# Reordering the first stage of a two-block transformer kernel: x in two loads, the memory row one unit earlier

## The reference, cut to what matters

```python
h = rmsnorm(x, norm_mix[i])
proj = h @ a_w_in[i]
u, b_gate, c_gate, q_mem = split(proj, [CONV_WIDTH, 2 * CONV_WIDTH, 3 * CONV_WIDTH])
v = c_gate * u
conv = w[0] * vp[:, 0:s] + w[1] * vp[:, 1:s + 1] + w[2] * vp[:, 2:s + 2]
y_tok = b_gate * conv
mem_kv = rmsnorm(mem, mem_norm) @ w_mem_kv[i]
```

## Time and profile of the kernel before

| | |
|---|---|
| median of 3 runs | 934.93 us (933.76 to 939.04) |
| the profiled execution | 932.69 us, of which the span is 931.0 us |
| TensorE busy | 919.3 us, 99% |
| VectorE busy | 704.0 us, 76% |
| ScalarE busy | 549.9 us, 59% |
| granted TensorE clock | 0.999 of full speed |

### The profile page before, as it was taken

How to read it: one execution, slowest core, us unless ns; L and a number is a source line. 1 busy time by engine, 2 the same in 40 slices (tenths; PEclk the granted TensorE clock), 3 DMA queues, 4 the chain that set the end, 5 groups by cost and what they waited for, 6 DMA issues and landing times.

```text
span 931.0 us, 16864 instructions
## 1 busy us (share of the span) xinstructions
PE 919.3 (99%) x6163; PEld 813.4 (87%) x6163; DVE 704.0 (76%) x1284; ACT 549.9 (59%) x969; POOL 81.9 (9%) x105
## 2 busy tenths in 40 slices
PE   8999999999999999999999999999999999999997
PEld 8999888888888987888888888999889789999985
DVE  4978777767666777687766677998687887688975
ACT  5654465545455677665555546775654745477883
POOL 0000011111110000100000000000011005622200
PEclk9999999999999999999999999999999999999999
DMA  8665557766666332667655663544231685423312
GB/s 322 210 204 178 191 172 238 224 215 200 207 204 190 112 113 92 234 224 229 206 191 183 189 187 118 174 146 134 83 102 50 202 286 189 142 87 102 119 46 91
DMA packets 43726, 157.94 MB, mean 170 GB/s; under 512 B 5464, under 2 KB 6248, under 8 KB 42896
## 3 DMA queue, kind: packets, MB, share of 16 engines
q1 hardware_dynamic: 41520, 147.79, 48.6%
q0 software_dynamic: 1856, 8.58, 2.5%
q10 hardware_dynamic: 288, 0.72, 0.3%
HBM read 155.63 MB, written 1.05 MB: 168 GB/s over the span
## 4 chain that ended last, share of the span: by engine, by line
PE 89%; DVE 5%; ACT 3%; DMA 2%; issue 1%; SPq 0%; DVEq 0%; ACTq 0%
PE ps L758 15%; PE ps L543 9%; PE ps L544 8%; PE ps L545 8%; PE ps L756 8%; PE ps L598 7%; PE ps L602 7%; PE ps L600 7%; PE ps L753 2%; DMA raw<-stream_dram 2%; PE ps L1145 1%; DVE wl L1772 1%; PE ps L754 1%; PE ps L1099 1%; ACT wh L1231 1%
## 5 line engine op out<-in xcount | busy, mean ns | idle before, releaser
L1772 DVE TENSOR_TENSOR wl<-raw,wh 128x1024 fp32r<-128x1024 f32 x270 | 331.8, 1234 | 100.0 <-ACT wh L1399 50.5
L1231 ACT ACTIVATE wh<-raw 128x1024 fp32r<-128x1024 f32 x174 | 182.0, 1056 | 91.6 <-DMA raw<-stream_dram 83.3
L758 PE MATMUL ps<-hxa,wh 128*128 128x512 f32 x616 | 219.6, 396 | 0.0
L543 PE MATMUL ps<-hxa,wh 128*128 128x256 f32 x672 | 196.6, 293 | 1.8 <-DVE hxa L1783 0.9
L544 PE MATMUL ps<-hxa,wh 128*128 128x256 f32 x672 | 189.9, 283 | 0.0
L545 PE MATMUL ps<-hxa,wl 128*128 128x256 f32 x672 | 189.8, 282 | 0.0
L756 PE MATMUL ps<-hxa,wl 128*128 128x256 f32 x616 | 171.9, 279 | 0.0
L543 PEld LDWEIGHTS ps<-hxa,wh 128*128 128x128 f32 x672 | 128.3, 191 | 11.3 <-issue 7.0
L1399 ACT ACTIVATE wh<-raw 128x1024 fp32r<-128x1024 f32 x96 | 101.6, 1058 | 59.9 <-PE ps L758 21.7
L758 PEld LDWEIGHTS ps<-hxa,wh 128*128 128x128 f32 x616 | 115.6, 188 | 24.0
L544 PEld LDWEIGHTS ps<-hxa,wh 128*128 128x128 f32 x672 | 128.6, 191 | 0.1
(11 more groups left out here) (370 smaller groups left out, 1354.2 us busy)
## 6 DMA issues: line engine op xcount, KB each, us to landing
raw<-stream_dram SPq DMA_DIRECT2D x271, 512.0 KB, 4.1
biasm<-bias_dram POOLq DMA_DIRECT2D x12, 192.0 KB, 4.2
w<-w_dram POOLq DMA_DIRECT2D x1, 2048.0 KB, 10.8
mlw<-mlw_dram POOLq DMA_DIRECT2D x1, 1056.0 KB, 6.9
x<-x_dram SPq DMA_DIRECT2D x1, 1024.0 KB, 7.2
mem<-memT_dram SPq DMA_DIRECT2D x1, 1024.0 KB, 8.3
memx<-mem_dram SPq DMA_DIRECT2D x1, 1024.0 KB, 5.8
grow<-rows_dram POOLq DMA_DIRECT2D x2, 512.0 KB, 4.5
```

The costliest lines, as they stand in the source:

```text
L543: pe.matmul(o, wh[:, w_s, w_cols], act[hi], start=start, stop=False, skip_group_check=True)
L758: return pe.matmul(o, wh[:, s % RING, wc], hx[:, k, :, :], start=False, stop=(k == KC - 1), skip_group_check=True)
L1231: act.activation(wh[:, v % RING, :], raw[:, v % RAW, :], ACT.Copy).then_inc(wh_ready, 1)
L1772: dve.tensor_tensor(wl[:, s % RING, :], raw[:, s % RAW, :], wh[:, s % RING, :].bitcast(F32), ALU.subtract).then_inc(wl_ready, 1)
```

## The change

- **SP:** x is loaded in two transfers of 512 KB, tokens 0 to 127 and 128 to 255, with unit 4 between them; each has its own semaphore.
- **ACT:** the first square stands ahead of the split of unit 4, the second behind it. The two squares and the root of `memx` move from step 6 to step 5 of the loop and stand ahead of the high part of convolution 0; the high part of a convolution stands behind them in its step.
- **DVE:** the token row and the two queries are taken in step 1, ahead of the first low parts of the memory (before: step 2). Each of the first two convolutions is computed behind the low part of the weight unit of the next step (before: ahead of it) and directly followed by its own low part. The memory's reciprocal and diagonal stand in step 6 behind the low part of unit 10 (before: step 7, ahead of unit 11, behind the take of b of convolution 1).
- **PE:** the memory's row is made behind unit 8 (before: behind unit 9).

```diff
             load(RAW, RAW)
             sp.dma_start(ident[:], ident_d).then_inc(ident_landed, 16)
-            sp.dma_start(x[:], x_d).then_inc(x_landed, 16)
+            sp.dma_start(x[:, 0, :], x_d[:, 0, :]).then_inc(x_landed[0], 16)
             load(RAW + 1, RAW + 1)
+            sp.dma_start(x[:, 1, :], x_d[:, 1, :]).then_inc(x_landed[1], 16)
             load(RAW + 2, RAW + 2)
...
-                if e == ("K", 0, 1):
+                if e == ("K", 0, 0):
                     rrow(ROW_MEM, 2)
...
-            for u in range(2, 5):
+            for u in range(2, 4):
                 split(u)
-            act.wait_ge(x_landed, 16)
-            for t in range(2):
-                square(Q_A, t, ajunk)
+            act.wait_ge(x_landed[0], 16)
+            square(Q_A, 0, ajunk)
+            split(4)
+            act.wait_ge(x_landed[1], 16)
+            square(Q_A, 1, ajunk)
             root2(Q_A, 0)
...
-                if j and A_PRE[j - 1][0] == "c":
-                    high(t_y[:], A_PRE[j - 1][1], A_PRE[j - 1][1])
-                if j == 6:
+                if j == 5:
                     act.wait_ge(memx_landed, 16)
...
+                if j and A_PRE[j - 1][0] == "c":
+                    high(t_y[:], A_PRE[j - 1][1], A_PRE[j - 1][1])
...
-                if j == 7:
-                    dve.wait_ge(mstd_ready, 1)
-                    dve.reciprocal(mrt, mstd).then_inc(mrt_ready, 1)
-                    dve.wait_ge(mrt_ready, 1)
-                    diagonal(mrt)
...
                 if j:
                     ahead_of(PA[e], e)
+                if j == 6:
+                    dve.wait_ge(mstd_ready, 1)
+                    dve.reciprocal(mrt, mstd).then_inc(mrt_ready, 1)
+                    dve.wait_ge(mrt_ready, 1)
+                    diagonal(mrt)
                 if e in (("u", 1), ("K", 0, 0)):
                     done = 0 if e[0] == "u" else 1
+                    convolve(done)
                     low_part(t_y[:], done, Y_A_SLOTS.index(done))
-                if j == 2:
+                if j == 1:
                     rows(ROW_A, 0, R)
```

More of the change, by code:

```diff
@@ L374, in build @@
         xT_landed = [sem(f"xT_landed{i}") for i in range(2)]
-        x_landed, grow1_landed, grow2_landed = sem("x_landed"), sem("grow1_landed"), sem("grow2_landed")
+        x_landed = [sem("x_landed%d" % t) for t in range(2)]
+        grow1_landed, grow2_landed = sem("grow1_landed"), sem("grow2_landed")
         mem_landed, cols_landed, ident_landed, consts_landed, bias_landed, bd_landed, mlw_landed, w1_landed = (
@@ L2026, in take_a, with convolve @@
                     take(c, {"u": t_u, "b": t_b, "c": t_c}[e[0]][:], R)
[L2027 to L2030, removed]
+            def convolve(j):
+                dve.wait_ge(proj_taken, PA["c", j].n + 1)
                 link(dve.tensor_tensor(cu[:, 2:T + 2], t_u[:], t_c[:], ALU.mult))
@@ L2039, in take_a, with take_fill_a @@
                     low_part(t_y[:], j, Y_A_SLOTS.index(j))
+            def take_fill_a(e):
+                take_a(e)
+                if e[0] == "c":
+                    convolve(e[1])
             for j, e in enumerate(A_PRE):
@@ L2065, in _ @@
                     take_a(e)
-            attend(*PAIRS_A, PA, A_FILL, take_a, PA_OUT)
+            attend(*PAIRS_A, PA, A_FILL, take_fill_a, PA_OUT)
             def gate_weights():
@@ L2072, in gate_weights @@
                 dve.tensor_tensor(gwl[:], gatew[:], gwh[:].bitcast(F32), ALU.subtract).then_inc(gw_ready, 1)
-            dve.wait_ge(x_landed, 16)
+            for t in range(2):
+                dve.wait_ge(x_landed[t], 16)
             ffn(PF0, 0, Q_FFN0, Y_FFN0, 0, PA_OUT["out", 7], "ffn0", 2, ROW_F0, gate_weights)
```

## The result

| | before | after |
|---|---|---|
| median | 933.58 us (20 runs) | 937.96 us (20 runs, 935.44 to 941.29) |
| ratio | 1 | 1.0044, 95% interval 1.0037 to 1.0052 |
| profiled execution: span | 931.0 us | 936.6 us |
| granted clock, whole span | 0.999 | 0.994 |
| start of the first scores | 46.80 us | 51.96 us |

The kernel became slower by 4.4 us, of which the forecast had 0.5. The loss lies where it was looked for, ahead of the first scores; the rest of the span is the same within 0.5 us. In the 20 runs the granted clock lay between 0.994 and 0.998. A change in the tables and sums is counted from 933.58 us, the median of 20 runs of the kernel before; the prediction had 3 of them, with a median of 934.93.

The account below looks back on a forecast made before the run. TensorE, 99% busy, was taken as the bound. Gains of 1.1 us at unit 4, 0.5 at the keys and a few tenths between, against a new 2.7 us pause, gave 934.93 + 0.5 = 935.4 us, range 932.8 to 938.0.

Parts of the forecast that it names:

- two rivals of about +2.0 each: Unit 9's landing holds VectorE (+2.0 us, chance 0.15); TensorE's clock falls in the new pause (+2.0 to +3.5, chance 0.13).
- the sign of the first: Unit 9's low part on VectorE starting later than 32.5 us would decide for the late-landing rival, chance 0.15.
- What bounds the kernel, and how much can be won: TensorE, busy 99%, bounds; only its four pauses before the first scores, 1.87 us together, can be won.
- x in halves: At unit 4 on TensorE: both pauses, 0.57 and 0.49 us, go, a gain of 1.11 us.
- The bound of 18.60 for its landing: Unit 4's load, issued between the halves of x, lands between 16.75 and 18.60 us, the latter meaning no gain.
- The memory's row behind unit 8: TensorE asks for the memory's diagonal at 35.43 us, VectorE has it at 38.1: a wait of 2.7 instead of 0.35 us.
- the low parts that release the loads all come 1 to 2 us earlier than before: Reason given for expecting no late landing of units 6 or 9, and so taking +0.5 from -0.4 to +2.0 us.
- the upper bound: Unit 9 landing at its old 31.92 us, its low part ready at about 33.0 + 1.2: +2.0 us at the scores.
- The cover for the convolution's low part: On VectorE, the low part directly behind the convolution waits for ScalarE's copy, 0.4 to 0.6 us, taken as 0.55.
- The clock: Rival: TensorE's clock halves in the new pause, a slow start costing 1.5 us, +2.0 to +3.5 in all; chance 0.13.
- The keys: Before the scores at 47.31 us: keys taken by 45.3, 2 us early, so the old pause of 0.46 us goes.
- No case reaches 0.5%: Whole run: a 4.7 us loss needs fallen clock and late landing together; within 0.5% given 0.91, slower 0.06.

Follow-up runs that it names:

- the control: The changed kernel, unchanged, run and profiled a second time beside other runs on the same chip: 937.87 us, ratio 1.0053 to the kernel before.
- e3: The kernel before with only x loaded in two halves and the two squares around unit 4's split: 934.64 us, ratio 1.0008.
- e7: The changed kernel with the load of unit 9 issued ahead of the load of memx: 936.08 us, ratio 1.0027 to the kernel before.
- e1: The changed kernel with only the memory's row put back behind unit 9: 934.31 us, ratio 1.001 to the kernel before.
- e2: The kernel before with only the memory's row moved to behind unit 8: 937.48 us, ratio 1.0039.
- e11: The changed kernel with convolutions, memx squares and memory's diagonal in their old order, the row still behind unit 8: 936.47 us, ratio 1.0033 to the kernel before.
- the two filled ones: The changed kernel with 20 unused products of ones in TensorE's pause before the memory's row, run twice: 936.90 and 939.02 us, ratios 1.0045 and 1.0049.

## Why the prediction was right or wrong

The time of 937.96 us lies 0.04 us inside the range of 932.8 to 938.0 us, and the change, 0.44% with an interval of 0.37 to 0.52%, was within 0.5%, as given with 0.91. That the time is inside is luck. The forecast stood on a median of 3 runs that was 1.35 us above the median of 20, and this hid a part of the error: counted as a change the range goes from -2.1 to +3.1 us, the forecast is +0.5, and measured are +4.4. The direction and the place of the loss were right, its size was not.

The error has two terms, and in the first profile they give it whole: the row product came at 40.69 instead of 38.15, +2.5 us, and the low clock cost +2.0, where the forecast had put it at nothing. With the +0.5 of the forecast that is 5.05 of the 5.16 us at the scores. In the control they are +1.7 (39.84) and +1.4, in all 3.6 of 3.67. In other words, two rivals of about +2.0 each, with chances of 0.15 and 0.13, came true together in the first profile. In the control the sign of the first (unit 9's low part later than 32.5) was there too, but by another cause.

- **What bounds the kernel, and how much can be won: right.** The whole difference lies ahead of the scores, 5.16 of 5.6 us of span, and nothing was won beyond the pauses that the trace had.
- **x in halves: right in the first profile, not in the control.** 1.01 us at the end of unit 8 in the one, 1.11 predicted, but 0.13 in the other, where unit 4 was split at 19.04, even behind the 18.60 of before. The bound of 18.60 for its landing did not hold there. What was missing is in e3: alone it gains nothing, since VectorE is next in line.
- **The memory's row behind unit 8: right in kind, wrong in size.** The pause is there, 5.16 us instead of 2.7 in the first profile and 3.43 in the control. The step that failed is the line "the low parts that release the loads all come 1 to 2 us earlier than before", by which I took the middle and not the upper bound. In the first profile unit 8 was issued 1.9 us earlier and landed 0.9 us later, unit 9 was issued as before and landed 0.9 us later; VectorE's low part of it started at 33.94, not by the 33.0 of the bound. e7 takes this wait away and brings the diagonal to 38.78. In the control the diagonal was late mostly because unit 4 was: VectorE copied the token row at 23.84 instead of the 22.70 of the forecast, and unit 9's low part started at 33.09 with no wait.
- **The cover for the convolution's low part: right.** 0.48 us idle, 0.55 taken.
- **The clock: its price right, its chance far too small.** 2.0 and 1.4 us, against 1.5 from the opening row. Of the profiles with a pause of 2.4 us or more at this place, all six without filler (the changed kernel and its control, e1, e2, e7, e11) have the low clock; in none of those with at most 0.8 us, nor in the two filled ones, was it low in this stage. I weighed that the old pauses had done nothing, but the longest of them was 0.57 us and so said nothing about 2.7. The Trainium skill, page "TensorE: Matmul & The Clock Gate", section "HAM oscillation — how this bites in real kernels", says that a wait between bursts of matmuls can throttle TensorE again, so that the next burst starts at half clock. The trace after agrees: 0.50 granted from 40 to 45 us.
- **The keys: right.** The scores follow without a wait.
- **No case reaches 0.5%: nearly wrong.** I took the low clock for a rival of its own, but it came with the pause itself, with the late landing or without it: e7, where unit 9 landed early, has a pause of 3.34 us and the low clock too. So the +1.4 to +2.0 belonged in the sum.

## What to carry to other kernels

Before a step on the critical engine is moved ahead, ask when its operand is ready, and put it where there is slack behind the operand, not where it can start soonest; the row one unit later, with its keys taken first, stood 2.0 to 2.6 us behind its diagonal in its three profiles and did not wait in any. An engine that works in order must not have the thing that lands last queued ahead of work that is ready. An earlier issue is not an earlier landing: with the DMA engines 92 to 97% busy unit 8 was issued 1.9 us earlier here and landed 0.9 us later, while the order of the loads did move a landing (e7). A pause of 2.4 us or more on TensorE cost its own length and a slower stretch behind it in all six such profiles here, so it is to be priced with both. And a forecast on a base of three runs has their scatter in it: compare the changes, not the times.

## What the runs showed of the hardware

- The granted clock fell to 0.50 in or behind pauses of 5.16, 3.3 to 3.7 and, in one profile, 2.4 us, and the matmuls of 128x256 then started 0.21 us apart instead of 0.12. The fall came within the pause in three of the six profiles, with the row product in e7, and about 1.5 us after TensorE was at work again in e1 and e2. The low stretch lasted about 3.4 us in four of them and 6.8 us in two, and it varied for one kernel: the control had 0.71 in the stretch from 40 to 45 us where the first profile had 0.50.
- Products of ones by ones, of no use to the computation, kept it at 1.00 over the same time in both profiles.
- The same load of 512 KB took 3.7 us from issue to landing in the kernel before and in the control, and 6.5 us in the first profile after (unit 8). The profiles of one kernel had unit 4 split at 17.64 and 19.04, unit 9 at 32.85 and 31.83.
- A wait of up to 2.0 us for GpSimd far behind the edits (at 807 to 811 us) comes and goes between runs of one kernel; of all profiles one had a low clock behind it too, and its rest of the span was 4.8 us longer than that of the same kernel without it.
